# End of a decoder-trunk kernel: who waits for the last stores, who issues them, and which squares the last channel sums read

## What is computed

```python
def _rmsnorm(x, g):
    xf = x.astype(jnp.float32)
    y = xf * lax.rsqrt(jnp.mean(xf * xf, axis=-1, keepdims=True) + EPS)
    return (y * g.astype(jnp.float32)).astype(x.dtype)

def _mlp(h, w1, w2):
    z = jax.nn.relu(h @ w1)
    return (z * z) @ w2

def reference(...):
    for i in range(DEPTH):
        ...
        xp = xp + _mlp(_rmsnorm(xp, norm_mlp[i]), mlp_w1[i], mlp_w2[i])
        xs = xs + _mlp(_rmsnorm(xs, norm_mlp[i]), mlp_w1[i], mlp_w2[i])
    y_prompt = _rmsnorm(xp, norm_final)
    y_sample = _rmsnorm(xs, norm_final)
```

## Time and profile before

| what | us |
|---|---|
| median of 3 runs | 1636.54 |
| lowest and highest of the 3 | 1633.74, 1638.12 |
| the profiled execution, device time | 1630.78 |
| its span, first to last instruction | 1629.0 |

### The profile page before, as it was taken

One profiled execution on the slowest core, in us unless ns is written; L12 is line 12 of the kernel. 1 busy time (PEld: TensorE's weight loads), 2 busy tenths in 40 slices (PEclk: granted clock), 3 DMA queues, 4 the chain that ended last, 5 costly groups with the idle time before them and its releaser, 6 DMA issues.

```text
span 1629.0 us, 31779 instructions
## 1 busy us (share of the span) xinstructions
PE 1516.3 (93%) x11325; PEld 1419.5 (87%) x11325; DVE 765.3 (47%) x1219; ACT 594.7 (37%) x1038; POOL 342.9 (21%) x398
## 2 busy tenths in 40 slices
PE   5988888879999899999999999789999999999995
PEld 5856666659889799999999999679999999999994
DVE  3765545554555354342334454874444432344332
ACT  6333443375555333321133323442233311233321
POOL 0274564424430102210022133020012200122000
PEclk9989999899999999999999999799999999999997
DMA  7122322422332322322222375603322232222221
GB/s 174 24 60 74 93 82 71 120 85 82 98 112 68 103 79 78 90 78 90 78 78 80 102 230 124 233 15 86 87 78 77 78 91 85 76 84 78 83 61 58
DMA packets 245278, 147.56 MB, mean 91 GB/s; under 512 B 42071, under 2 KB 239614, under 8 KB 244190
## 3 DMA queue, kind: packets, MB, share of 16 engines
q1 hardware_dynamic: 238114, 139.39, 29.3%
q0 software_dynamic: 6704, 7.20, 1.8%
q10 hardware_dynamic: 396, 0.13, 0.0%
HBM read 128.42 MB, written 18.26 MB: 90 GB/s over the span
## 4 chain that ended last, share of the span: by engine, by line
PE 80%; DVE 5%; issue 5%; ACT 2%; POOL 1%; POOLq 1%; DMA 0%; SPq 0%; DVEq 0%; ACTq 0%
PE bank L852 58%; PE bank L772 5%; PE bank L965 4%; PE bank L1091 3%; PE bank L1056 3%; PE bank L915 2%; PE bank L932 1%; PE bank L978 1%; PE bank L972 1%; DVE arena_parts L1800 1%; DVE tmpa L2275 1%; ACT arena L1346 1%; DVE arena L2302 1%; DVE sq L2275 1%; PE bank L992 0%
## 5 line engine op out<-in xcount | busy, mean ns | idle before, releaser
L852 PE MATMUL bank<-arena_parts,wR 128*128 128x288 f32 x4224 | 565.1, 295 | 7.8 <-ACT arena_parts L1415 3.7
L852 PEld LDWEIGHTS bank<-arena_parts,wR 128*128 128x128 f32 x4224 | 560.7, 188 | 10.2 <-issue 6.8
L852 PE MATMUL bank<-side_parts,wR 128*128 128x288 f32 x3360 | 447.2, 295 | 1.1 <-DVE tmpa L2347 1.1
L852 PEld LDWEIGHTS bank<-side_parts,wR 128*128 128x128 f32 x3360 | 445.4, 188 | 1.5 <-issue 1.3
L1814 DVE TENSOR_TENSOR wR<-wraw,wR 128x1024 fp32r<-128x1024 f32 x159 | 232.7, 1464 | 237.9 <-ACT wR L1409 236.5
L1409 ACT ACTIVATE wR<-wraw 128x1024 fp32r<-128x1024 f32 x159 | 167.0, 1050 | 201.9 <-PE bank L852 187.5
L735 POOL TENSOR_TENSOR arena_parts<-sq,arena_parts 128x576 f32 x64 | 91.6, 1432 | 674.1 <-ACT arena_parts L1627 674.1
L1346 ACT ACTIVATE arena<-bank 128x256 f32<-128x256 f32 (+9 forms) x223 | 95.7, 445 | 155.6 <-PE bank L972 65.8
L1624 ACT ACTIVATE tmpa<-bank 128x576 f32<-128x576 f32 x64 | 41.7, 652 | 195.4 <-PE bank L852 195.4
L2198 DVE TENSOR_TENSOR sq<-tmpa 128x576 f32<-128x576 f32 x64 | 48.5, 758 | 127.1 <-ACT tmpa L1624 127.1
L772 PE MATMUL bank<-ident,arena 128*128 128x128 f32 (+4 forms) x400 | 69.2, 293 | 19.5 <-DVE arena L1980 15.4
(11 more groups left out here) (295 smaller groups left out, 1500.9 us busy)
## 6 DMA issues: line engine op xcount, KB each, us to landing
wraw<-in_mlp_w SPq DMA_DIRECT2D x128, 512.0 KB, 3.9
side<-in_cache_ckv SPq DMA_DIRECT2D x128, 128.0 KB, 2.1
wraw<-in_ssm_w_glu SPq DMA_DIRECT2D x16, 512.0 KB, 3.9
s_state_to_out<-side SPq DMA_DIRECT2D x16, 256.0 KB, 2.5
s_in_to_state<-yblk SPq DMA_DIRECT2D x8, 512.0 KB, 2.6
s_in_to_out<-side SPq DMA_DIRECT2D x64, 64.0 KB
wraw<-in_mla_w_o SPq DMA_DIRECT2D x8, 512.0 KB, 5.2
side<-s_in_to_state SPq DMA_DIRECT2D x2, 2048.0 KB, 12.7
```

The lines of the kernel that those rows point to most:

```text
L852: return pe.matmul(bank[:, a, 0:HALF], wR[:, s, wp, k, :], tokens(k, xp)[:, a * HALF:(a + 1) * HALF], start=(first and j == 0), stop=(last ...
```

## The change

It does three things.

1. POOL no longer waits for the stores of y; SP does, as its last instruction.
2. SP issues the stores of blocks 0, 1 and 4 only. ACT issues those of blocks 2 and 3, after it has scaled both.
3. The channel sums are split in two. PE first multiplies `acc`, which holds tiles 0 to 6, with the ones (five matmuls into `bank23`, right behind the last product), then turns the last gained tile, then adds the sums of the last tile's squares, read from `sq` directly (five more matmuls into the same columns). DVE no longer adds the last square to `acc`. On ACT the copies of the last turned tile now stand ahead of the square roots.

```diff
-            for j in (0, 2, 1, 3, 4):
-                if j in (2, 3):
-                    sp.wait_ge(fin_ya, j - 1)
-                else:
-                    sp.wait_ge(fin_y, {0: 1, 1: 2, 4: 3}[j])
+            for j in (0, 1, BLK):
+                sp.wait_ge(fin_y, {0: 1, 1: 2, BLK: 3}[j])
                 dst = O["y_prompt"][0, j * P:(j + 1) * P, :] if j < BLK else O["y_sample"].rearrange("b q n -> (b q) n")
                 rows = P if j < BLK else NS
                 sp.dma_start(dst, ynat[0:rows, j, :]).then_inc(y_out, 16)
+            sp.wait_ge(y_out, 16 * (BLK + 1))
...
             pool.wait_ge(out_sem, 16 * (5 + 4))
-            pool.wait_ge(y_out, 16 * (BLK + 1))
...
+            def token_sums(src, first, last):
+                for j in range(BLK + 1):
+                    n = P if j < BLK else NS
+                    ins = pe.matmul(bank23[0:n, 0, j:j + 1], src[:, j * P:j * P + n], ones[:, 0:1],
+                                    start=first and j == 0, stop=last and j == BLK, skip_group_check=True)
+                return ins
+
             mlp(1)
+            pe.wait_ge(sq_used, Q_END - 1)
+            pe.wait_ge(tile_free, T_OUT - 1)
+            token_sums(acc, True, False)
             tokens_down(KT - 1)
-
-            pe.wait_ge(sq_used, Q_END)
-            for j in range(BLK):
-                pe.matmul(bank01[:, 0, j:j + 1], acc[:, j * P:(j + 1) * P], ones[:, 0:1], start=True, stop=True)
-            pe.matmul(bank01[0:NS, 0, BLK:BLK + 1], acc[:, SEQ:N], ones[:, 0:1], start=True, stop=True)\
-                .then_inc(ss_done, 1)
+            pe.wait_ge(sq_ready, Q_END)
+            token_sums(sq[:, 1, :], False, True).then_inc(ss_done, 1)
...
             mlp(1)
+            tokens_down(KT - 1)
             act.wait_ge(var_ready, 4)
             act.activation(stat[:, 0:BLK], stat[:, 0:BLK], ACT.Sqrt)
             act.activation(stat[0:NS, BLK:BLK + 1], stat[0:NS, BLK:BLK + 1], ACT.Sqrt).then_inc(rstd_ready, 1)
-            tokens_down(KT - 1)
             act.wait_ge(rstd_ready, 4)
             act.wait_ge(fin_sb, KT)
             for j in (2, 3):
                 act.activation(ynat[:, j, :], ynat[:, j, :], ACT.Copy, scale=stat[:, j:j + 1]).then_inc(fin_ya, 1)
+            for j in (2, 3):
+                act.wait_ge(fin_ya, j - 1)
+                act.dma_start(O["y_prompt"][0, j * P:(j + 1) * P, :], ynat[:, j, :]).then_inc(y_out, 16)
...
-                            if half == 1:
+                            if half == 1 and not (isinstance(it, int) and i == 1 and it * 2 + j == KT - 1):
                                 add_square(it * 2 + (q0 + j), j)
```

More of the change, by code:

```diff
@@ L2354, in _ @@
             dve.wait_ge(ss_done, 6)
-            own(dve.tensor_scalar(stat[:, 0:BLK], bank01[:, 0, 0:BLK], 1.0 / D, EPS, ALU.mult, ALU.add))
-            own(dve.tensor_scalar(stat[0:NS, BLK:BLK + 1], bank01[0:NS, 0, BLK:BLK + 1], 1.0 / D, EPS, ALU.mult, ALU.add))
+            own(dve.tensor_scalar(stat[:, 0:BLK], bank23[:, 0, 0:BLK], 1.0 / D, EPS, ALU.mult, ALU.add))
+            own(dve.tensor_scalar(stat[0:NS, BLK:BLK + 1], bank23[0:NS, 0, BLK:BLK + 1], 1.0 / D, EPS, ALU.mult, ALU.add))
             settle()
```

## The result

The changed kernel takes 1625.38 us in the median of five runs (1621.99 to 1627.94); the kernel before takes 1633.74, also in the median of five (1630.78 to 1638.12). Those five are the three runs known before, one more of 1633.50, and the profiled execution. The ratio is 0.9943, 95% interval 0.9920 to 0.9965: faster by 8.4 us in the medians. In a later comparison, all on one chip, the ratio was 0.9964 (0.9948 to 0.9981). The profiled execution of the changed kernel took 1621.99 us with a span of 1620.3; it is the fastest of its five.

The account below looks back on a forecast made before the run. PE, busy 93%, was taken as the bound, leaving only the 23.2 us chain behind the last product to change. Wait 6.3 + norm 1.2 + stores nothing = 7.5 us; 1636.54 - 7.5 = 1629.0 us, range 1625.0 to 1632.0.

Parts of the forecast that it names:

- POOL's drain and its cover: Program's end: POOL's 6.69 us drain moves beside earlier work, over some 110 us before the barrier; worth 6.3 us.
- an end that keeps its price: Program's end, rival: SP's drain costs what POOL's did, or the 6.7 us exist only when profiled; 1635.3 us, chance 0.14.
- The norm: Last product to first scaling: split sums and earlier copy bring the first scaling 1.2 us earlier, at 1612.14 against 1613.34.
- The rival with the held clock: Norm after the last product: first sums keep the clock up, scaling 2.1 us earlier; 1628.1 us, chance 0.15.
- The cover of the first sums: Behind the last product: first ten sums take 2.17 us inside PE's 2.45 us wait, 0.28 to spare.
- The stores: Stores of y, two issued on ACT: the stream stays full and ends 7.7 us after its first issue; worth nothing.
- the 3.5 that they had: ACT's two store issues: 1.6 + 1.9 = 3.5 us before the stream of stores runs dry.
- the base of 1636.54: Whole kernel: median of three timed runs, from which the 7.5 us gain was subtracted to give 1629.0 us.
- the 0.87 at the end: Stores' landing to span's end: 0.2 waking and branching, 0.37 SP drain, 0.3 barrier, in place of 7.2 us.
- the seven signs: Profile after: POOL's drain, SP's wait and drain, span's end, ten sums, copy order, first scaling near 1612.1, DMA without gap.

Follow-up runs that it names:

- the three executions at half clock: Profiled: the changed kernel once more (ratio 0.9964), the kernel before with split sums and copy order alone (1.0001), the changed kernel with four more POOL drains (tail 15.3 us).
- the added drains: Changed kernel with four more drains in POOL's program: one before its DMAs, one behind 128 key loads, two behind its last computation; tail 15.3 us.

## Why the prediction was right, and where it was not

**The mechanism was right.** The prediction put 6.3 of 7.5 us on POOL's drain and its cover, and the experiments give 6.8 in the tail and 6.4 in timed runs for just that wait. The term is 0.5 short because of two small values at its end. SP's drain was taken as 0.37 from the earlier trace rows and is 0.007: the row of before was a drain straight behind the issues, while now it stands behind a wait that has seen them land. (All executions agree: 368 to 370 ns where SP does not wait, 7 ns where it does.) SP's wake to the end is 0.3 to 0.4 in all, where the sum had 0.87.

Of the drain itself the prediction said that nothing in the trace tells what it waits for, and kept 0.14 for an end that keeps its price. The experiments narrow it down: the first drain behind a stretch of POOL's own DMAs and computations pays, one with nothing in between does not, wherever POOL's wait stands. Which of the two it pays for stays open. The page of the Trainium skill that the prediction weighed against this (VectorE: DVE Perf Modes, section The DRAIN you can't avoid) has some 12 ns for the drains that the runtime puts around a program. SP's 7 ns here and the 43 to 53 ns of a second drain of POOL are near that, POOL's first one is not. But lines 101 and 2404 are lines of the kernel, so these drains are the kernel's own and may not be the ones that the page means; the page is weaker ground for the rival than the prediction took it for.

**The norm was right at the half clock.** 1.2 was forecast, with the second sums starting when the transposes' loads end; the three executions at half clock give 1.1, and the loads start at 1613.47, 0.05 behind the transposes' (1612.55 + 0.87). The rival with the held clock, 2.1 and a chance of 0.15, is what the profiled execution of the changed kernel shows, at 2.4: I had scaled the sums, from their first load to the end of their last matmul, from 2.17 to 1.51, and they take 1.26 (1609.33 to 1609.36 + 1.23). The ratio was off: it was read from transposes of 0.57 and 0.82, but the clock fell in the course of the second ones. In the kernel before it was 0.82 in the mean of the half microsecond in which they begin, between the 1.00 and the 0.50 of the earlier trace rows:

```profile
1608.00:1608.50 0.50, 0.29 (x2) 0.29 (x3) 0.00 (x0) 0.50 (x2) 0.00 (x0) 0.82 0.00 0
```

Where one clock holds throughout, these loads take 0.50 at the full and 0.87 to 0.88 at the half clock, and those of the sums 1.18 to 1.20 and 2.13, both near a factor of 0.56. The cover of the first sums was larger than reckoned, 1.46 us instead of 0.28, since they ran at the full clock in all four executions; the earlier trace rows had 1.00 in that stretch already, and the sum took the half clock's 2.17 for it all the same.

**The stores were right:** nothing, and ACT's issues, 1.41 for two, were inside the 3.5 that they had.

**What failed is the size of two terms: the base of 1636.54, and the 0.87 at the end.** 1625.38 was measured, 1629.0 predicted; it lies 0.4 us above the lower end of the range. Of the 3.6 us, 2.8 are the base: the prediction took its gain from 1636.54, the median of three runs, and two more put that median at 1633.74. One of the two is the profiled execution of 1630.78, which the prediction had before it. It had seen that this execution lay 5.8 below the median, and explained only why the gain should not scale, not which of the two numbers was the likelier base. Which median a few runs give is in part luck: in the two later comparisons, on a chip each, the kernel before had 1635.41 (23 runs) and 1631.05 (27 runs).

The other 0.9 is the gain, 8.4 in the medians against 7.5. Here the step that failed is the stretch from the last landing to the span's end: 0.87 in the sum, 0.3 to 0.4 measured, so that the wait is worth 6.8 and not 6.3. At the full clock the norm's term was too small as well, 1.2 in the sum and 2.4 measured. The tail gives a gain of 7.9 at the half clock (23.2 to 15.3) and 9.2 at the full one; the two timed comparisons give 9.3 and 5.9 by their ratios, too far apart to tell 7.5 from 7.9 or 9.2.

Of the seven signs that the prediction named, six came: POOL's drain at 1503.7 to 1511.6, SP's wait over at 1620.0 and its drain short, the span's end within 0.4 us of the wake, ten sums ahead of the transposes, the copies ahead of the root, and stores without a gap (365 to 410 GB/s in each microsecond from 1613 to 1618). The seventh did not: the first scaling came 5.16 us behind the last product, where the forecast had 6.38 (1612.14 - 1605.76) and the rival with the held clock 5.47.

## What to carry to other kernels

Read the program's last microseconds by queues, not by busy engines: 7.2 us of this kernel held no computation and no transfer, only a drain on an engine that had finished 117 us earlier. Where GpSimd has issued DMAs of its own, let it reach its end, or an extra drain, while other engines still work, and give the last wait to an engine whose drain is short behind it (7 ns on SP here). And compare such changes by the tail, from a fixed event to the end: the timed runs scatter by more than two of the three parts were worth.

## What the runs showed of the hardware that was not expected

A drain of POOL took 6.7 to 8.7 us (5.3 to 8.0 without the rest of a computation that it waited for) the first time behind a stretch in which POOL had issued DMAs and computed, even hundreds of microseconds after its last issue, and 0.04 to 0.05 us the next time.

Whether the clock falls in the norm is not set by the instructions alone: with the same PE program it was 1.00 through the second sums in one execution and 0.50 in three. PE had been idle for 1.46 us, behind ten matmuls of a single column, in all four.

The scatter of the timed runs goes with the granted clock: over the 23 and the 27 runs of the kernel before, time and mean clock have a correlation of -0.91 and -0.80. And in the profiled executions it lies for the most part ahead of the tail. Span and mean granted clock of three executions of the changed kernel, not all on one chip, the third with the added drains, which lie beside other work:

```profile
core 0: 1620.3 us, clock 0.974
core 0: 1623.8 us, clock 0.971
core 0: 1626.9 us, clock 0.966
```

Between the first and the third 6.6 us lie in the span, of which 1.3 in the tail; the last product ended at 1606.31 in the one and at 1611.56 in the other.
